# Down-projection tiles of a four-layer decoder on one core: twenty products of 256 columns become ten of 512, four stay

## The chip, the cores and the metric

The kernel runs on one core of one Trainium2 chip. The metric is the device time of one execution, in microseconds (us), and lower is better.

## The reference

Four post-norm layers over 256 tokens of 1024 channels. Each layer is a token mixer (forgetting attention, S5, mean pooling, forgetting attention again) and a SwiGLU feed-forward part with 2816 hidden channels; both are added to the residual and normalised. The change touches only the last factor of the feed-forward part.

```python
def swiglu(x, w1, w3, w2):
    return (jax.nn.silu(x @ w1) * (x @ w3)) @ w2

for i in range(DEPTH):                       # 4 layers
    m = mixer(h)                             # fox, s5, pool, fox
    h = layer_norm(DN_ALPHA * h + m, ln_g[i, 0], ln_b[i, 0])
    h = layer_norm(DN_ALPHA * h + swiglu(h, ffn_w1[i], ffn_w3[i], ffn_w2[i]), ln_g[i, 1], ln_b[i, 1])
```

## The kernel before, in words

**Split operands.** Every large product is made of three. Weights and activations are float32; each is split into a high part in the type that TensorE takes (fp32r) and a low part, the rest. The kernel sums high·high, high·low and low·high into the same PSUM bank.

**Weights.** They come as 370 tiles of 128 x 1024 floats in the order of their use. SyncE's queue brings a tile into one of four `raw` buffers; ScalarE writes its high part (line 617), VectorE its low part (line 1021), into a ring of places called `whi`/`wlo` (four places) and `ext` (up to four more, high and low). TensorE tells with the semaphore `w_used` when the last product of a tile is through, and the place is free.

**The feed-forward part.** The 2816 hidden channels are 22 chunks of 128. For a chunk c, `up1(c)` and `up3(c)` use one weight tile each: helper `fm` makes 24 products (8 blocks of 128 input channels, three products each, lines 1628 to 1630). In these, a 128 x 128 block of the *weight* is loaded into the array (the stationary operand), and 256 columns of the split activation `xboth`, all tokens, are streamed (the moving operand), into bank 4 or 5. ScalarE and VectorE make silu and gate, and split the result into `hhi` (line 703) and `hlo`, two buffers that alternate by chunk. The last two chunks of a layer have buffers of their own, `h3hi`/`h3lo` and `h4hi`/`h4lo`.

`down(c)` multiplies a chunk of h with its tile of w2 and adds to the accumulators of the layer, banks 0 to 3: tokens 0 to 127 in banks 0 and 1, tokens 128 to 255 in banks 2 and 3, 512 output channels in each. Here it is *h* that is loaded into the array, 128 hidden channels x 128 tokens, and the weight that is streamed. It goes through helper `tm_quarters` (line 1660): for each token half m, for each of the three pairs (a, w), four products of 256 columns, 24 in a tile. All other tiles of this orientation (attention's v and output, S5, the pool's output) go through `tm_half`, which makes the same sums with products of 512 columns, 6 for a token half. The last three chunks of a layer, four in the last layer, go through `tm_end`, also in products of 512 columns (line 1692), ordered bank by bank. So `tm_quarters` serves 19 chunks in each of the first three layers and 18 in the last.

**Order of the work.** It is written out by hand, per engine. In a layer's feed-forward part TensorE runs

```python
                for c in range(3, FCH):
                    up1(c)
                    up3(c)
                    if c < FCH - 3:
                        down(c - 1)
```

with `down(0)` and `down(1)` together ahead of it. `down` waits for its weight tile's low part (`w_lo`) and for h's low part (`hlo_ready`), and its last product raises `w_used`. In the first layer, eight blocks of transposes for S5 tables (line 1842) follow downs.

**Where things lie in SBUF.** The buffers are placed one behind another, and small fillers set their starts. Modulo 512 bytes, `whi`, `wlo`, `ext`, `ohi`, `olo` (the mixers' split outputs) and `h3hi` to `h4lo` start at 0; `xboth` starts at 448; `hhi` and `hlo` start at 64. A stationary operand of 128 floats is 512 bytes wide in each partition.

Of the kernel before, what the change touches and what calls it, by code (L numbers as in the profile page):

```python
# [27 lines left out]
P = 128  # L28
SEQ = 256
D = 1024  # L30
KC = D // P
TM = SEQ // P
HALF = 512
# [71 lines left out]
def build(nc, t, layers=DEPTH, last_ffn=True):  # L105
# [39 lines left out]
    with ExitStack() as ctx:  # L145
# [92 lines left out]
        def hi_of(c):  # L238

            p = place[c]  # L240
            return whi[:, p, :] if p < SPL else ext_hi[:, p - SPL, :] if p < SPL + EXT else far_hi[:, :]

        def lo_of(c):

            p = place[c]
            return wlo[:, p, :] if p < SPL else ext_lo[:, p - SPL, :] if p < SPL + EXT else far_lo[:, :]
# [1344 lines left out]
        def _(pe):  # L1591
            mm = nc.tensor.matmul
# [40 lines left out]
            def tm_half(c, m, a_hi, a_lo, banks, first, last=False, lo_ready=None):  # L1633

                cols = slice(m * P, (m + 1) * P)
                for j in range(2):
                    mm(banks[2 * m + j][:, :], a_hi[:, cols], hi_of(c)[:, j * HALF:(j + 1) * HALF], start=first, stop=False)  # L1637
                for j in range(2):
                    mm(banks[2 * m + j][:, :], a_hi[:, cols], lo_of(c)[:, j * HALF:(j + 1) * HALF], start=False, stop=False)  # L1639
                if lo_ready is not None:  # L1640
                    pe.wait_ge(xT_ready, lo_ready)
                for j in range(2):
                    ins = mm(banks[2 * m + j][:, :], a_lo[:, cols], hi_of(c)[:, j * HALF:(j + 1) * HALF], start=False, stop=last)  # L1643
                return ins
# [8 lines left out]

            def tm_quarters(c, a_hi, a_lo, banks, first):

                for m in range(TM):
                    cols = slice(m * P, (m + 1) * P)
                    for a, w, start in ((a_hi, hi_of(c), first), (a_hi, lo_of(c), False), (a_lo, hi_of(c), False)):
                        for q in range(4):
                            ins = mm(banks[2 * m + q // 2][:, q % 2 * SEQ:(q % 2 + 1) * SEQ], a[:, cols], w[:, q * SEQ:(q + 1) * SEQ],  # L1660
                                     start=start and q % 2 == 0, stop=False)
                return ins

            def tm_first(c, banks):
# [138 lines left out]
            def ffn(l, n):  # L1803
# [24 lines left out]
                def down(c):  # L1828
                    t = T0 + down_at(c)
                    pe.wait_ge(w_lo, t + 1)  # L1830
                    pe.wait_ge(hlo_ready, E0 + (2 if c < 2 else c + 1))
                    used(tm_quarters(t, hhi[:, c % 2, :], hlo[:, c % 2, :], acc, c == 0))
# [534 lines left out]
```

## Time and profile before

| | |
|---|---|
| median of three runs | 1169.89 us (1168.87 to 1171.18) |
| the profiled execution, its own time | 1169.65 us |
| its span, first to last instruction | 1167.9 us |
| TensorE busy | 1150.9 us, 99% |
| VectorE busy | 819.2 us, 70% |
| ScalarE busy | 601.4 us, 51% |
| matrix products (MATMUL records) | 9166 |
| mean granted TensorE clock | 0.999 |

The profiled execution's time is the span and 1.75 us around it. Matrix products are pipelined: the duration of a record (279 ns for 256 columns) is longer than the distance to the next start, so what a product costs is read from starts and not from durations. The timeline prints starts to 0.01 us; over the 24 products of a tile that is within half a nanosecond for each.

### The profile page before, as it was taken

The page shows a single profiled execution, that of the slowest core. Times are in us where ns is not written, and L with a number is a line of the kernel's source. Part 1 is how long each engine was busy: PE and PEld are TensorE (multiplying, and loading weights), DVE is VectorE, ACT ScalarE, POOL GpSimd, SP SyncE. Part 2 cuts the span into 40 slices and gives each one's busy share as a digit, 9 for nine tenths or more (in the row PEclk, how much of TensorE's full clock was granted, in tenths as well). Part 3 has the DMA queues.
Part 4 walks back from the last instruction along what each step waited for, and adds up shares of the span by engine and source line. Part 5 has one row for each costly group of instructions (what it writes and reads, how often), then busy time and mean ns, then how long its engine had stood idle before and what let it go on. Part 6 is the DMA issues. An engine that isn't in the chain of part 4 may idle for free.

```text
span 1167.9 us, 22245 instructions
## 1 busy us (share of the span) xinstructions
PE 1150.9 (99%) x9166; PEld 1068.3 (91%) x9166; DVE 819.2 (70%) x1263; ACT 601.4 (51%) x947; POOL 161.3 (14%) x212
## 2 busy tenths in 40 slices
PE   8999999999999999999999999999999999999997
PEld 7998899999977779999998899999989988999996
DVE  7789899989868687455466776554587768654545
ACT  6777544544445456354444555444438664644441
POOL 0650099002970000000000000000010000000000
PEclk9999999999999999999999999999999999999999
DMA  6676454554756558565654556656536334856540
GB/s 243 219 269 228 160 198 151 193 181 175 235 167 211 181 180 300 178 226 180 202 170 162 198 180 236 201 180 205 190 101 241 130 109 146 277 188 200 182 163 37
DMA packets 63981, 221.14 MB, mean 189 GB/s; under 512 B 8068, under 2 KB 9988, under 8 KB 63368
## 3 DMA queue, kind: packets, MB, share of 16 engines
q1 hardware_dynamic: 57224, 202.57, 50.8%
q0 software_dynamic: 5648, 15.73, 4.1%
q8 instruction: 73, 1.20, 0.4%
q10 hardware_dynamic: 1008, 1.41, 0.4%
q14 instruction: 28, 0.23, 0.1%
HBM read 211.03 MB, written 7.60 MB: 187 GB/s over the span
## 4 chain that ended last, share of the span: by engine, by line
PE 93%; DVE 4%; DMA 1%; ACT 1%; issue 1%; SPq 0%; DVEq 0%; ACTq 0%
PE bank L1660 18%; PE bank L1628 15%; PE bank L1629 15%; PE bank L1630 15%; PE bank L1758 5%; PE bank L1692 4%; PE bank L1637 3%; PE bank L1643 3%; PE bank L1639 3%; DMA raw<-in_w 1%; PE bank L1949 1%; PE bank L1608 1%; PE bank L1793 1%; PE bank L1931 1%; PE bank L1960 1%; PE bank L1948 1%
## 5 line engine op out<-in xcount | busy, mean ns | idle before, releaser
L1021 DVE TENSOR_TENSOR wlo<-raw,whi 128x1024 fp32r<-128x1024 f32 x227 | 288.3, 1277 | 61.2 <-ACT whi L617 60.3
L617 ACT ACTIVATE whi<-raw 128x1024 fp32r<-128x1024 f32 x227 | 239.0, 1056 | 76.5 <-PE bank L1660 29.1
L1628 PE MATMUL bank<-xboth,whi 128*128 128x256 f32 x936 | 261.3, 279 | 0.0
L1629 PE MATMUL bank<-xboth,whi 128*128 128x256 f32 x936 | 259.3, 277 | 0.0
L1630 PE MATMUL bank<-xboth,wlo 128*128 128x256 f32 x936 | 259.2, 277 | 0.0
L1021 DVE TENSOR_TENSOR ext<-raw,ext 128x1024 fp32r<-128x1024 f32 x142 | 172.3, 1222 | 42.3 <-ACT ext L617 42.1
L1628 PEld LDWEIGHTS bank<-xboth,whi 128*128 128x128 f32 x936 | 176.2, 188 | 1.1 <-issue 0.9
L1629 PEld LDWEIGHTS bank<-xboth,whi 128*128 128x128 f32 x936 | 175.9, 188 | 0.1
L1630 PEld LDWEIGHTS bank<-xboth,wlo 128*128 128x128 f32 x936 | 175.8, 188 | 0.0
L617 ACT ACTIVATE ext<-raw 128x1024 fp32r<-128x1024 f32 x142 | 148.9, 1056 | 45.8 <-PE bank L1660 22.5
L1628 PE MATMUL bank<-xboth,ext 128*128 128x256 f32 x600 | 167.2, 279 | 0.0
L1629 PE MATMUL bank<-xboth,ext 128*128 128x256 f32 x600 | 166.0, 277 | 0.0
L1630 PE MATMUL bank<-xboth,ext 128*128 128x256 f32 x600 | 166.0, 277 | 0.0
L1169 DVE TENSOR_TENSOR hval<-bank,silu 128x256 f32<-128x256 f32 x80 | 33.8, 423 | 159.8 <-PE bank L1630 159.7
L1628 PEld LDWEIGHTS bank<-xboth,ext 128*128 128x128 f32 x600 | 112.8, 188 | 0.9 <-issue 0.9
L1629 PEld LDWEIGHTS bank<-xboth,ext 128*128 128x128 f32 x600 | 112.8, 188 | 0.1
L1630 PEld LDWEIGHTS bank<-xboth,ext 128*128 128x128 f32 x600 | 112.7, 188 | 0.0
L703 ACT ACTIVATE hhi<-hval 128x256 fp32r<-128x256 f32 x72 | 30.0, 417 | 127.5 <-DVE hval L1169 125.4
L698 ACT ACTIVATE silu<-bank 128x256 f32<-128x256 f32 x80 | 30.5, 381 | 99.3 <-PE bank L1630 99.3
L584 POOL DMA_DIRECT2D slot<-in_ln_row x16 | 8.6, 545 | 446.0 <-DVE x_tm L1093 395.7
L1660 PE MATMUL bank<-ext,hhi 128*128 128x256 f32 x448 | 61.8, 281 | 0.0
L1660 PE MATMUL bank<-whi,hlo 128*128 128x256 f32 x376 | 59.6, 281 | 0.0
(383 smaller groups left out, 2036.1 us busy)
## 6 DMA issues: line engine op xcount, KB each, us to landing
raw<-in_w SPq DMA_DIRECT2D x370, 512.0 KB, 4.3
slot<-in_ln_row POOLq DMA_DIRECT2D x16, 512.0 KB, 5.1
toep<-slot POOLq DMA_DIRECT2D x8, 512.0 KB, 8.5
toepA<-toep SPq DMA_DIRECT2D x2, 1024.0 KB, 6.5
BT<-toep SPq DMA_DIRECT2D x2, 1024.0 KB, 7.3
x_tm<-in_x SPq DMA_DIRECT2D x2, 512.0 KB, 5.2
slot<-in_s_B SPq DMA_DIRECT2D x2, 512.0 KB, 5.6
slot<-in_s_C SPq DMA_DIRECT2D x2, 512.0 KB, 5.8
```

The costliest lines, as they stand in the source:

```text
L617: nc.scalar.activation(hi_of(c), raw[:, c % RAW, :], ACT.Copy).then_inc(w_hi, 1)
L1021: V.tensor_tensor(lo_of(c), raw[:, c % RAW, :], hi_of(c).bitcast(F32), ALU.subtract).then_inc(w_lo, 1)
L1169: V.tensor_tensor(hval[:, :], bank[5][:, 0:SEQ], silu[:, :], ALU.mult).then_inc(h_ready, 1)
L1628: mm(dst, wh, bhi[:, kc, :], start=(i == 0), stop=False)
L1629: mm(dst, wh, blo[:, kc, :], start=False, stop=False)
L1630: ins = mm(dst, wl, bhi[:, kc, :], start=False, stop=(i == len(chunks) - 1))
L1637: mm(banks[2 * m + j][:, :], a_hi[:, cols], hi_of(c)[:, j * HALF:(j + 1) * HALF], start=first, stop=False)
L1639: mm(banks[2 * m + j][:, :], a_hi[:, cols], lo_of(c)[:, j * HALF:(j + 1) * HALF], start=False, stop=False)
L1643: ins = mm(banks[2 * m + j][:, :], a_lo[:, cols], hi_of(c)[:, j * HALF:(j + 1) * HALF], start=False, stop=last)
L1660: ins = mm(banks[2 * m + q // 2][:, q % 2 * SEQ:(q % 2 + 1) * SEQ], a[:, cols], w[:, q * SEQ:(q + 1) * SEQ], start=start and q % 2 == 0, s ...
L1692: return mm(banks[b][:, :], (a_lo if lo_act else a_hi)[:, cols], (lo_of if lo_w else hi_of)(c)[:, half], start=False, stop=stop)
L1758: return mm(out, x[:, kc, m * P:(m + 1) * P], w[:, 0:4, kc * P:(kc + 1) * P], start=start, stop=stop)
```

## The change

`tm_quarters` is rewritten. The first token half goes through `tm_half`: six products of 512 columns. In the second, high·high and high·low are two products of 512 columns each, and low·high, the last, stays four products of 256 columns. The sums are the same, and added to each bank in the same order. A tile has 14 products in place of 24. Buffers, waits and the other engines' instructions are not touched.

```diff
             def tm_quarters(c, a_hi, a_lo, banks, first):
 
-                for m in range(TM):
-                    cols = slice(m * P, (m + 1) * P)
-                    for a, w, start in ((a_hi, hi_of(c), first), (a_hi, lo_of(c), False), (a_lo, hi_of(c), False)):
-                        for q in range(4):
-                            ins = mm(banks[2 * m + q // 2][:, q % 2 * SEQ:(q % 2 + 1) * SEQ], a[:, cols], w[:, q * SEQ:(q + 1) * SEQ],
-                                     start=start and q % 2 == 0, stop=False)
+                tm_half(c, 0, a_hi, a_lo, banks, first)
+                cols = slice(P, 2 * P)
+                for a, w, start in ((a_hi, hi_of(c), first), (a_hi, lo_of(c), False)):
+                    for j in range(2):
+                        mm(banks[2 + j][:, :], a[:, cols], w[:, j * HALF:(j + 1) * HALF], start=start, stop=False)
+                for q in range(4):
+                    ins = mm(banks[2 + q // 2][:, q % 2 * SEQ:(q % 2 + 1) * SEQ], a_lo[:, cols], hi_of(c)[:, q * SEQ:(q + 1) * SEQ],
+                             start=False, stop=False)
                 return ins
```

On TensorE, a down tile in the middle of the first layer's feed-forward part, with the end of the up tile ahead of it (lines 1628 to 1630) and the start of the next. Before:

```order
L1628 MATMUL bank<-xboth,whi 128x256
L1629 MATMUL bank<-xboth,whi 128x256
L1630 MATMUL bank<-xboth,wlo 128x256
L1660 MATMUL bank<-whi,hhi 128x256 x4
L1660 MATMUL bank<-wlo,hhi 128x256 x4
L1660 MATMUL bank<-whi,hlo 128x256 x4
L1660 MATMUL bank<-whi,hhi 128x256 x4
L1660 MATMUL bank<-wlo,hhi 128x256 x4
L1660 MATMUL bank<-whi,hlo 128x256 x4
L1628 MATMUL bank<-xboth,whi 128x256
L1629 MATMUL bank<-xboth,whi 128x256
```

With the change:

```order
L1628 MATMUL bank<-xboth,whi 128x256
L1629 MATMUL bank<-xboth,whi 128x256
L1630 MATMUL bank<-xboth,wlo 128x256
L1637 MATMUL bank<-whi,hhi 128x512 x2
L1639 MATMUL bank<-wlo,hhi 128x512 x2
L1643 MATMUL bank<-whi,hlo 128x512 x2
L1660 MATMUL bank<-whi,hhi 128x512 x2
L1660 MATMUL bank<-wlo,hhi 128x512 x2
L1662 MATMUL bank<-whi,hlo 128x256 x4
L1628 MATMUL bank<-xboth,whi 128x256
L1629 MATMUL bank<-xboth,whi 128x256
```

Nothing changes its place: five groups of four products of 256 columns have become five of two products of 512, and the group ahead of the next up tile is as it was. The lines 1637, 1639 and 1643 are those of `tm_half`.

## Rows read from the trace of the kernel before

**Rows 1.** The page: busy time of TensorE, and the chain that ended last
```profile
PE 1150.9 (99%) x9166; PEld 1068.3 (91%) x9166; DVE 819.2 (70%) x1263; ACT 601.4 (51%) x947; POOL 161.3 (14%) x212
...
PE bank L1660 18%; PE bank L1628 15%; PE bank L1629 15%; PE bank L1630 15%; PE bank L1758 5%; PE bank L1692 4%; PE bank L1637 3%; PE bank L1643 3%; PE bank L1639 3%; DMA raw<-in_w 1%; PE bank L1949 1%; PE bank L1608 1%; PE bank L1793 1%; PE bank L1931 1%; PE bank L1960 1%; PE bank L1948 1%
```
**Rows 2.** Waits of TensorE: us in total, times, longest; the two largest
```profile
PE bank L1608 <- DVE x_tm L1093: 2.7, 3, 1.1
PE bank L1668 <- ACT whi L617: 1.8, 1, 1.8
```
**Rows 3.** Line 1660, weight loads and products: ns min/median/max, first and last start
```profile
L1660 PEld LDWEIGHTS bank<-ext,hhi x448: 187/188/192, 459.7 to 1131.9; 128*128 128x128 f32 x150
L1660 PE MATMUL bank<-ext,hhi x448: 277/281/281, 459.8 to 1132.0; 128*128 128x256 f32 x150
...
L1660 PE MATMUL bank<-whi,hhi x376: 277/281/281, 145.3 to 1114.9; 128*128 128x256 f32 x188
...
L1660 PE MATMUL bank<-wlo,hhi x376: 281/281/281, 145.8 to 1115.4; 128*128 128x256 f32 x188
...
L1660 PE MATMUL bank<-whi,hlo x376: 281/281/283, 146.2 to 1115.9; 128*128 128x256 f32 x188
...
L1660 PE MATMUL bank<-ext,hlo x224: 281/281/282, 460.8 to 1132.5; 128*128 128x256 f32 x112
```
**Rows 4.** Timeline of PE (start us, us of the group): down tile, two up tiles, down
```profile
164.69 0.63 PE L1660 MATMUL bank<-whi,hhi 128*128 128x256 f32 x4
...
167.51 0.29 PE L1628 MATMUL bank<-xboth,whi 128*128 128x256 f32 x1
...
170.25 0.28 PE L1628 MATMUL bank<-xboth,whi 128*128 128x256 f32 x1
...
172.97 0.63 PE L1660 MATMUL bank<-whi,hhi 128*128 128x256 f32 x4
```
**Rows 5.** Timeline of PE, last layer's end: 512 columns, h stationary
```profile
1148.92 0.62 PE L1692 MATMUL bank<-ext,hhi 128*128 128x512 f32 x2
1149.37 0.40 PE L1692 MATMUL bank<-ext,hlo 128*128 128x512 f32 x1
1149.61 0.63 PE L1692 MATMUL bank<-ext,hhi 128*128 128x512 f32 x2
1150.08 0.39 PE L1692 MATMUL bank<-ext,hlo 128*128 128x512 f32 x1
1150.31 0.39 PE L1692 MATMUL bank<-whi,h3hi 128*128 128x512 f32 x1
...
1151.69 0.63 PE L1692 MATMUL bank<-ext,hhi 128*128 128x512 f32 x2
1152.16 0.40 PE L1692 MATMUL bank<-ext,hlo 128*128 128x512 f32 x1
...
1153.09 0.39 PE L1692 MATMUL bank<-whi,h3hi 128*128 128x512 f32 x1
```
**Rows 6.** Timeline of PE, attention output of the last layer: 512 columns, ohi stationary
```profile
963.19 0.61 PE L1639 MATMUL bank<-wlo,ohi 128*128 128x512 f32 x2
...
964.55 0.61 PE L1639 MATMUL bank<-wlo,ohi 128*128 128x512 f32 x2
...
966.82 0.62 PE L1692 MATMUL bank<-ext,ohi 128*128 128x512 f32 x2
967.27 0.39 PE L1692 MATMUL bank<-ext,olo 128*128 128x512 f32 x1
```
**Rows 7.** Timeline of PE, v to first q: tile of 512, then two up-like tiles
```profile
34.98 0.28 PE L1628 MATMUL bank<-xboth,whi 128*128 128x256 f32 x1
...
37.73 0.28 PE L1628 MATMUL bank<-xboth,whi 128*128 128x256 f32 x1
```
**Rows 8.** Timeline of PE, pool layer: 24 products of 256 between tiles of 512
```profile
652.05 0.62 PE L1643 MATMUL bank<-whi,xboth 128*128 128x512 f32 x2
652.51 0.28 PE L1628 MATMUL bank<-ohi,whi 128*128 128x256 f32 x1
...
655.39 0.40 PE L1637 MATMUL bank<-ext,xboth 128*128 128x512 f32 x1
```
**Rows 9.** Windows of those stretches: length, PE busy, PEclk, DMA share, GB/s
```profile
162.00:172.00 10.00, 10.00 (x90) 1.00 0.59 203
650.00:656.00 6.00, 6.00 (x39) 1.00 0.84 279
959.00:968.00 9.00, 9.00 (x45) 1.00 0.46 152
1148.92:1160.05 11.13, 11.13 (x50) 1.00 0.00 0
```

## The prediction, made before the changed kernel was run

> **What bounds the kernel now.** I read the page first. TensorE is busy for 1150.9 us of a span of 1167.9, and the chain that ended last runs through its products, 18% of it through line 1660, the one that changes [rows 1]. I then asked what TensorE waits for: the largest entries are 2.7 us and 1.8 us over the whole program, and neither is at line 1660 [rows 2]. So in the feed-forward parts no other engine or transfer is late. The time there is the sum of the distances between starts of products, and a nanosecond saved in a down tile is a nanosecond saved at the end. The granted clock is 1.00 in every stretch that I use, which is 2.4 GHz, so streaming alone is 256 / 2.4 = 106.7 ns or 512 / 2.4 = 213.3 ns [rows 9].
>
> The reader is to see next that starts say more than durations. A weight load's record takes 188 ns and a product's 281 [rows 3], yet a down tile, 24 products, goes from 164.69 to 167.51, in 2.82 us, so 117.5 ns a product [rows 4]. Loads and products overlap their neighbours. The excess over streaming is 10.8 ns a product. The up tiles beside it do better: the one right after the down tile takes 2.74 us (167.51 to 170.25), the second 2.72 (170.25 to 172.97), or 113.3 ns a product [rows 4].
>
> **How many tiles.** Line 1660 has 448 + 376 + 376 + 376 + 224 = 1800 products [rows 3], 24 in a tile, so 75 down tiles. They take 75 x 2.82 = 211.5 us, 18% of the span, which is what the chain says.
>
> **The change, part by part.**
>
> *Twenty products of 256 columns go.* At 117.5 ns each they are 2.350 us of a tile.
>
> *Ten of 512 columns come.* Before has no such product inside a down tile, but it has the same operands at a layer's end: `hhi` and `hlo` loaded, a tile of w2 streamed, 512 columns. The first six of them, right after an up tile, take 1148.92 to 1150.31 = 1.39 us; six later ones take 1151.69 to 1153.09 = 1.40 us, 233.3 ns each [rows 5]. These are the nearest rows, the same operands at the same addresses. A down tile also starts after an up tile, so I take 1.39 for its first six and 4 x 0.2333 = 0.933 for the next four: 2.323 us.
>
> *The bounds of this price.* From below: with `ohi` loaded, which starts at a multiple of 512 bytes, six take 963.19 to 964.55 = 1.36 us, 226.7 ns each [rows 6]; ten are 2.267 us. From above: the slowest pair with `hhi` is 0.47 us (1149.61 to 1150.08, 1151.69 to 1152.16), 235 ns a product [rows 5]; ten are 2.350 us, exactly what they replace. I take the value with h loaded, because the difference between the rows with `ohi` and with h goes with what is loaded, and that does not change.
>
> *Four of 256 stay.* 4 x 0.1175 = 0.470 us. They now follow a product of 512 columns. The price of that change of width is not in the trace for h; the nearest row is an up-like tile behind one of 512 columns: 34.98 to 37.73 = 2.75 us [rows 7], against 2.74 behind a down tile of 256 columns and 2.72 behind an up tile [rows 4]. So the change of width costs 0.01 us at most beyond what the change of operands costs anyway. Bounds: 0 and 0.03. I take 0.01.
>
> *The step to the next up tile.* The last four products are as before, so its first tile keeps its 2.74 us. Cost 0.
>
> *Everything else.* 750 products and 750 loads are no longer issued (a tile has 14, not 24); TensorE's records fall from 9166 to 8416. No wait, buffer, DMA or instruction of another engine is added. `down` still waits for `hlo_ready` and `w_lo`, which are never late [rows 2], and its last product still raises `w_used`, with 0.02 us less behind its first. Nothing hides this edit's terms, since the whole tile lies on the path that ends last; each counts in full. What could come late next is the weights' supply: three tiles of 512 KB in 164.69 to 172.97, 8.28 us, are 190 GB/s, and the same queues move 279 GB/s in another stretch [rows 4, 9]. 0.02 us in 8.28 do not touch that.
>
> *The sum.* A new tile: 1.39 + 0.933 + 0.470 + 0.01 = 2.803 us; an old one 2.82. The gain is 0.017 us, 0.02 at the precision of the starts, and x 75 = 1.5 us. Against the profiled execution's 1169.65 us (span 1167.9) that is 1168.2. The median of the runs stands 0.24 us above that execution, so I forecast 1169.89 - 1.5 = **1168.4 us**. 0.2% of it, 2.3 us, is about what a measurement of this kernel can tell from no change, so the forecast is "the same", a little on the fast side.
>
> **A rule weighed against the rows.** What a product costs beyond its streaming is 10.8 ns at 256 columns with h loaded and 233.3 - 213.3 = 20.0 ns at 512 [rows 4, 5]; for an aligned operand it is 226.7 - 213.3 = 13.4 ns at 512 [rows 6]. It almost doubles with the width, so it is nearly a share of the streaming (8 to 10%), and only some 2 ns a product (2 x 117.5 - 233.3 = 1.7) are a fixed price that wider products save. The Trainium skill, in "TensorE: Matmul & The Clock Gate", section "Wait — 56ns, not 53.3ns?", says that a warm product costs its columns over the clock and a fixed part behind decode, about 2.5 ns, whatever the width. By that figure, a tile would save 10 x 2.5 = 25 ns and the kernel 1.9 us; but by the same rule a tile of 24 would take 24 x 109.2 = 2620 ns, and the trace has 2820. So the rule does not account for most of the excess here. If that excess were fixed as well, the change would be worth more; this is rival B.
>
> **The rivals.**
>
> *A, aligned pace.* The products of 512 columns alternate banks, as in `tm_half`, where layer ends run several products in a row into one bank. If that order and not h's place set the 233.3 ns, they would run at 226.7 [rows 6]. A tile is 2.267 + 0.470 + 0.01 = 2.747 us, 0.073 less, 5.5 us in all: 1164.4 us. For it: the six rows of `ohi` at 226.7 are of `tm_half`, and those of h are not. Against: `ohi` keeps that pace in `tm_end`'s order too, where a pair takes 966.82 to 967.27 = 0.45 us, and h there takes 0.47 [rows 5, 6]. So far the pace follows the operand and not the order.
>
> *B, the excess is fixed per product.* A product of 512 would take 213.3 + 10.8 = 224.1 ns, a tile 10 x 0.2241 + 0.470 = 2.711 us, a gain of 0.109 or 8.2 us: 1161.7 us. For it: nothing but the rule quoted above, in whose terms this is. Against: no row of 512 columns anywhere is under 226 ns [rows 5, 6].
>
> *C, slower: the loads fall out of step and the following up tile pays.* In the pool layer, right behind products of 512 columns, 24 products of 256 take 652.51 to 655.39 = 2.88 us, 120 ns each, and never come back to 113.3 [rows 8]. If the mixed widths put the first up tile behind each down tile into that pace, it would take 2.88 and not 2.74: 0.14 x 75 = 10.5 us, less the 1.5 gained: 1178.9 us. It makes the kernel slower by over 0.2% from 0.05 us a tile on, that is from about eight products at 120 ns on. Against: in the pool's stretch `ohi` is streamed and not `xboth`, and behind 512 columns `xboth` recovers within the tile (2.75 us) [rows 7]; and the four narrow products lie between.
>
> *D, the upper bound.* Ten products at 235 ns and 0.02 for the change of width: 2.350 + 0.470 + 0.02 = 2.840, 0.02 more a tile: 1171.4 us. A matter of how six-product patterns fall, not of another mechanism.
>
> *E, the change does nothing at all,* because the tile's end is set by something else: 1169.9 us. Against: the waits.
>
> **How the numbers follow.** The forecast's case (a gain of 0 to 0.04 us a tile) has 0.62, A 0.12, B 0.05, C 0.09, D 0.08, E 0.04. In the forecast's case a fifth lies beyond 2.3 us of gain, 0.12; with A and B that makes faster 0.29. Slower is C and a quarter of D, 0.11. Same is the rest, 0.60. The range goes from 1164.3, which takes in A, to 1171.4, the bound D; B, C and some chance beyond are left out, under 2 in 10.
>
> **What would show it.** In the changed kernel's timeline a down tile should take 2.80 us (2.79 to 2.81) from the first product of line 1637 with h to the first of line 1628; the pair of products on lines 1637, 1639 and 1643 0.46 to 0.47 us; the last four 0.47 to 0.48; the up tiles behind 2.74 and 2.72. Pairs of 0.45 us would show A or B; an up tile of 2.8 or more, C. A wait of TensorE in the feed-forward parts of more than a microsecond in all, or a down tile outside 2.74 to 2.84 us, would make the reasoning wrong.

## The result, and the profile after

The changed kernel takes 1176.29 us, median of eight runs (1172.16 to 1177.33), against 1170.15 us for the kernel before (eight runs, 1167.84 to 1171.39). The ratio is 1.0046, 95% interval 1.0035 to 1.0056: slower by about 5.4 us, where 1.5 us less was forecast, and outside the range that ended at 1171.4. The profiled execution took 1174.88 us, its span is 1173.1, 5.2 more than before. The spread of the runs is worth a look: 5.2 us in eight, and 9.5 us (1170.61 to 1180.12) in twelve later ones, where the kernel before spreads over 3.6 us in eight.

The page of the changed kernel, answering to [rows 1], has the 8416 products that were expected, and TensorE is as busy as before:

```profile
PE 1157.6 (99%) x8416; PEld 1040.5 (89%) x8416; DVE 818.5 (70%) x1263; ACT 600.5 (51%) x947; POOL 160.2 (14%) x212
...
PE bank L1628 14%; PE bank L1629 14%; PE bank L1630 14%; PE bank L1660 6%; PE bank L1637 6%; PE bank L1643 6%; PE bank L1639 6%; PE bank L1760 5%; PE bank L1694 4%; PE bank L1662 3%; DMA raw<-in_w 2%; DVE wlo L1021 2%; PE bank L1608 1%; PE bank L1795 1%; DVE ext L1021 1%
```

So the time is still in TensorE's products, and the question is in which. The timeline of TensorE in the second layer (start us, us of the group), a down tile, the two up tiles and the next down tile, answers to [rows 4]:

```profile
466.53 0.62 PE L1637 MATMUL bank<-whi,hhi 128*128 128x512 f32 x2
...
468.86 0.64 PE L1662 MATMUL bank<-whi,hlo 128*128 128x256 f32 x4
469.33 0.29 PE L1628 MATMUL bank<-xboth,whi 128*128 128x256 f32 x1
...
472.07 0.28 PE L1628 MATMUL bank<-xboth,whi 128*128 128x256 f32 x1
...
474.79 0.39 PE L1637 MATMUL bank<-ext,hhi 128*128 128x512 f32 x1
```

Here all is as forecast: the down tile 2.80 us, the up tiles 2.74 and 2.72. The same view of the same execution in the third layer:

```profile
701.35 0.63 PE L1637 MATMUL bank<-ext,hhi 128*128 128x512 f32 x2
...
704.15 0.28 PE L1628 MATMUL bank<-xboth,ext 128*128 128x256 f32 x1
...
706.98 0.28 PE L1628 MATMUL bank<-xboth,whi 128*128 128x256 f32 x1
...
709.81 0.40 PE L1637 MATMUL bank<-whi,hhi 128*128 128x512 f32 x1
```

The down tile takes 2.80 us again, but both up tiles take 2.83: 118 ns a product in place of 113.3, for the same instructions with the same operands at the same clock. Every up tile of the feed-forward part behind a down tile of layers three and four is like this. In layer two none is: only its first takes 2.82 us, behind a stall, and the next is at 2.72 again. I call the two lengths the fast and the slow pace. A slow layer costs (0.09 + 0.11) us in each of its 19 passes, 3.8 us; two of them 7.6. The down tiles, 2.796 us where they were 2.823, give back 75 x 0.027 = 2.0.

A second, smaller loss is at two layers' starts. In these windows (length, PE busy, PEclk, DMA share, GB/s) TensorE was idle for 0.43 and 0.57 us:

```profile
448.00:457.00 9.00, 8.57 (x60) 1.00 0.89 297
692.00:701.00 9.00, 8.43 (x63) 1.00 0.86 279
```

There a weight tile lands late, ScalarE's split of it stands ahead of silu in its queue, and `up1(3)` waits for silu. The kernel before has no such wait in that profile, but the margin was small: in its third layer silu ended at 696.38 us and `up1(3)` began at 696.90. The rest, 5.2 - 7.6 + 2.0 - 1.0 = -1.4 us, lies elsewhere, mostly where nothing was changed: the first feed-forward part began 0.5 us earlier, and the stretch between the first and the second was 0.9 us shorter. In the first layer two things nearly cancel: three passes are slow, and end so at the first table transposes, but behind the transposes all up tiles are fast, where the kernel before has four slow pairs.

### The profile page after: what moved, and what is told of

Its sections match the earlier page's. It is cut to its first block, busy times and chain, and to the rows that moved or that the text cites. A ratio compares the mean times of both kernels' runs of the same rounds, so it can differ in the third digit from the quotient of the medians.

```text
span 1173.1 us, 20745 instructions
## 1 busy us (share of the span) xinstructions
PE 1157.6 (99%) x8416; PEld 1040.5 (89%) x8416; DVE 818.5 (70%) x1263; ACT 600.5 (51%) x947; POOL 160.2 (14%) x212
## 3 DMA queue, kind: packets, MB, share of 16 engines
q10 hardware_dynamic: 1008, 1.41, 0.4%
## 4 chain that ended last, share of the span: by engine, by line
PE 87%; DVE 8%; ACT 2%; DMA 2%; issue 1%; SPq 0%; ACTq 0%; DVEq 0%
PE bank L1628 14%; PE bank L1629 14%; PE bank L1630 14%; PE bank L1660 6%; PE bank L1637 6%; PE bank L1643 6%; PE bank L1639 6%; PE bank L1760 5%; PE bank L1694 4%; PE bank L1662 3%; DMA raw<-in_w 2%; DVE wlo L1021 2%; PE bank L1608 1%; PE bank L1795 1%; DVE ext L1021 1%
## 5 line engine op out<-in xcount | busy, mean ns | idle before, releaser
L627 ACT ACTIVATE xboth<-bank 128x256 fp32r<-128x256 f32 x64 | 21.2, 381 | 45.3 <-PE bank L1608 45.2
L1173 DVE TENSOR_TENSOR hlo<-hval,hhi 128x256 fp32r<-128x256 f32 x72 | 34.2, 475 | 0.0
```

## The experiments

**A second look at the same program.**

> The changed kernel once more, for a second profile of the same program. The first profile has up tiles (24 products of 256 columns) of two lengths: 2.72 to 2.74 us, as before the change, or 2.83 us, and in the third and fourth layer all of them are of the second kind. Theory I (inherited pace): the pace is set where a layer's feed-forward part begins, by how the starts happen to fall, and the new down tile hands it on. Then a second execution may have another set of layers at 2.83 us, and its time moves by some 4 us for each such layer. Theory II (the mixed tile itself is slow in these layers, by its places in the ring or by its addresses): the same layers and tiles at 2.83 us as in the first profile, and the same time, 1176 us.

Measured: 1175.99 us (twelve runs, ratio 1.0039, 1.0022 to 1.0055); the profiled execution 1171.54 us. Its third layer, slow in the first profile, is fast in this one:

```profile
709.83 0.62 PE L1637 MATMUL bank<-whi,hhi 128*128 128x512 f32 x2
...
712.63 0.29 PE L1628 MATMUL bank<-xboth,whi 128*128 128x256 f32 x1
...
715.37 0.28 PE L1628 MATMUL bank<-xboth,whi 128*128 128x256 f32 x1
...
718.09 0.39 PE L1637 MATMUL bank<-ext,hhi 128*128 128x512 f32 x1
```

2.80, 2.74 and 2.72 us. Of layers two to four only the last is slow in it, 38 up tiles of 38, and the profiled execution was 3.3 us quicker than the first. The program is the same to the byte, so addresses and ring places alone do not decide. Theory II falls.

**One old tile a layer.**

```diff
-                    used(tm_quarters(t, hhi[:, c % 2, :], hlo[:, c % 2, :], acc, c == 0))
+                    used((tm_narrow if c == 2 else tm_quarters)(t, hhi[:, c % 2, :], hlo[:, c % 2, :], acc, c == 0))
```

(`tm_narrow` is the old `tm_quarters`.)

> The change, but chunk 2 of each layer goes through the old down tile of 24 narrow products (4 tiles of 75). Theory I (inherited pace; 24 narrow products bring the following up tiles back to the fast pace, as every down tile did before, and 10 wide and 4 narrow ones do not): the up tiles of a layer are fast from chunk 4 on in all layers, some 8 us less than the changed kernel, 1168 to 1169.5 us. Theory II (the mixed tile makes the following up tile slow by itself): slow up tiles of 2.83 us come back behind the next mixed tile, about 1175 us.

Measured: 1168.63 us (eleven runs, 1166.72 to 1170.71), ratio to before 0.9981 (0.9971 to 0.9991). Timeline of TensorE at the start of its last layer; line 1672 is the old tile's:

```profile
998.43 0.28 PE L1628 MATMUL bank<-xboth,whi 128*128 128x256 f32 x1
...
1001.26 0.28 PE L1628 MATMUL bank<-xboth,whi 128*128 128x256 f32 x1
...
1004.09 0.63 PE L1672 MATMUL bank<-whi,hhi 128*128 128x256 f32 x4
...
1006.91 0.29 PE L1628 MATMUL bank<-xboth,whi 128*128 128x256 f32 x1
...
1009.65 0.28 PE L1628 MATMUL bank<-xboth,ext 128*128 128x256 f32 x1
...
1012.38 0.39 PE L1637 MATMUL bank<-ext,hhi 128*128 128x512 f32 x1
```

The layer starts slow (2.83, 2.83), one old tile of 2.82 us follows, and from then on the up tiles take 2.74 and 2.73, through 15 further mixed tiles. The first layer does the same; the second and third were fast when their old tile came, so the old tile ends the slow pace in two cases of two. A single mixed tile between up tiles neither makes the slow pace nor ends it. At a layer's start, where two of them follow each other, it is different (see the part on why the prediction was wrong). Replacing 4 tiles of 75 turned the change from 5 us slower into 2 us faster, which is about the gain that had been forecast for it.

**Kicks.** One idle product ahead of the down tile in two passes of layers 1 to 3 (counted from 0), in either kernel:

```diff
                     up3(c)
+                    if l > 0 and c in (8, 14):
+                        idle_products(7, 128)
```

> The changed kernel with one idle product of 128 columns (identity times a constant, into bank 7, which nothing reads) ahead of the down tiles in the passes of chunks 8 and 14 of layers 1 to 3; it adds under 0.3 us each. Theory I (inherited pace): the kick can move the starts from one pattern to the other, and what it leaves stays: the up tiles' length (2.72/2.74 or 2.83 us) changes at a kick and nowhere else within a layer. Theory II (places or addresses): the lengths do not care for the kicks.

Measured: 1172.95 us, one run. In the third layer, at chunk 8 (line 1730 is the kick, two records in the trace):

```profile
740.00 0.28 PE L1628 MATMUL bank<-xboth,whi 128*128 128x256 f32 x1
...
742.83 0.28 PE L1628 MATMUL bank<-xboth,ext 128*128 128x256 f32 x1
...
745.66 0.38 PE L1730 MATMUL bank<-cst 128*128 128x128 f32 x2
...
748.69 0.29 PE L1628 MATMUL bank<-xboth,ext 128*128 128x256 f32 x1
...
751.43 0.28 PE L1628 MATMUL bank<-xboth,ext 128*128 128x256 f32 x1
```

Up tiles of 2.83 us ahead of it, of 2.74 behind it, and fast to the layer's end. The last layer did the same. The second layer was fast, and both its kicks left it so. The pace changes at a kick and stays, as theory I has it; but the kick only led from slow to fast, which it had not said.

> The kernel before with the same kicks. Theory I: a down tile of 24 narrow products brings the fast pace back, so all up tiles of layers 1 to 3 behind a down tile stay at 2.74 and 2.72 us, kicks or not; the time is that of before and some 1 to 2 us. If up tiles of 2.83 us stay behind a kick here too, the old down tile does not restore the pace, and the theory falls.

Measured: 1172.27 us, one run. No up tile behind a kick is slow. This agrees, but tells less than hoped: no layer was in the slow pace when its kick came, so nothing had to be restored.

**h at multiples of 512 bytes.**

```diff
-        sb("behind_x", [P, 32])
+        sb("behind_x", [P, 16])
...
-        sb("behind_turn", [P, 4])
+        sb("behind_turn", [P, 20])
```

> The changed kernel with h's halves (and silu, hval and the tiles that share their place) 64 bytes lower, at multiples of 512 bytes; nothing else differs. If the pace of a wide product follows the address of what is loaded, as ohi's rows (226.7 ns) against h's (233.3 ns) say: the ten wide ones take 2.27 us and a down tile about 2.74 to 2.75 us in place of 2.80, 4 us less if the up tiles stay as they are in the changed kernel. If the address of h does not matter: down tiles of 2.80 us and no change. Open is what the up tiles do: fast throughout would give 1164 us, slow throughout 1180 us.

Measured: 1165.13 us (five runs, 1164.23 to 1165.60), ratio 0.9948 (0.9936 to 0.9960). Second layer:

```profile
498.53 0.63 PE L1637 MATMUL bank<-ext,hhi 128*128 128x512 f32 x2
...
500.81 0.64 PE L1662 MATMUL bank<-ext,hlo 128*128 128x256 f32 x4
501.29 0.29 PE L1628 MATMUL bank<-xboth,whi 128*128 128x256 f32 x1
...
504.03 0.28 PE L1628 MATMUL bank<-xboth,whi 128*128 128x256 f32 x1
```

The tile takes 2.76 us and the up tile 2.74; the ten wide products are 2.28 of it, 228 ns each, near [rows 6] and not [rows 5]. No layer of this execution stays slow. The second began with up tiles of 2.90 and 2.83 us behind a late start, and was fast from the next pass on, so this tile can end the slow pace; that is one case. The first and last layers, which began without delay, were fast from their first up tile.

A control moved silu and hval alike, and left h at 64 bytes above:

```diff
-        sb("behind_x", [P, 32])
+        sb("behind_x", [P, 16])
...
         hval = sb("hval", [P, SEQ])
+        sb("before_h", [P, 16])
```

> A control for the runs with h at 512: the changed kernel with silu and hval moved 64 bytes down as there, but h's halves left at 64 bytes above multiples of 512. If h's own address gave the 2.754 us tile and the return to the fast pace, this run is the changed kernel again: down tiles of 2.80 us, whole layers of up tiles at one pace or the other, 1170 to 1180 us by execution. If the neighbours' addresses did it: down tiles of 2.75 us and about 1165 us.

Measured: 1175.15 us, ratio 1.0039 (1.0022 to 1.0055). Down tiles of 2.80 us (706.08 to 708.88), layers two and four wholly slow. It is the changed kernel again, so h's own address is what counts, and not that of silu and hval. The kernel before got the same two changes of fillers as the first of these runs, its 24 narrow products kept:

> The kernel before (24 narrow products) with h's halves at multiples of 512 bytes. The pool layer's narrow products with operands at such addresses take 120 ns each, so if the address of what is loaded sets the pace: down tiles of 24 x 0.120 = 2.88 us and not 2.82, 4 us more, 1174 to 1175 us. If narrow products gain as the wide ones did: under 2.78 us and under 1168 us.

Measured: 1171.37 us (ten runs), ratio 1.0013 (0.9998 to 1.0028). The down tile is longer, as the first branch says, by 0.04 us and not 0.06; the time, for which it said 1174 to 1175 us, is not clear of no change:

```profile
508.45 0.63 PE L1660 MATMUL bank<-whi,hhi 128*128 128x256 f32 x4
...
511.31 0.29 PE L1628 MATMUL bank<-xboth,whi 128*128 128x256 f32 x1
```

2.86 us for 24, against 2.82 with h at 64. Inside the tile, narrow products lose by the address that wide ones gain by. The 75 tiles lose 2.8 us; 0.8 us come back in the first layer, where no up tile behind the transposes is slow in this run and four pairs were before. Whoever tried addresses with narrow products alone would find nothing to gain by leaving 64, and whoever tried widths at 64 alone would find narrow ones no worse.

**All products wide.**

```diff
-                    used(tm_quarters(t, hhi[:, c % 2, :], hlo[:, c % 2, :], acc, c == 0))
+                    used(tm(t, hhi[:, c % 2, :], hlo[:, c % 2, :], acc, c == 0, False))
```

> All products of a down tile 512 columns wide (12 of them), so the four last ones of 256 are gone as well. Theory I: a tile of 2.79 to 2.80 us, and the pace of the up tiles is handed on as well, so up tiles of 2.74/2.72 or 2.83 us by layer, time between 1168 and 1180 us by how many layers are slow. Theory III (it is the mix of widths in one tile that puts the loads out of step): up tiles 2.75 and 2.72 us everywhere, 1168 us.

Measured: 1174.14 us (seven runs, only 1173.24 to 1174.49), ratio 1.0022 (1.0012 to 1.0032). Last layer:

```profile
1037.17 0.28 PE L1628 MATMUL bank<-xboth,ext 128*128 128x256 f32 x1
...
1039.91 0.28 PE L1628 MATMUL bank<-xboth,ext 128*128 128x256 f32 x1
...
1045.42 0.28 PE L1628 MATMUL bank<-xboth,ext 128*128 128x256 f32 x1
...
1048.25 0.28 PE L1628 MATMUL bank<-xboth,whi 128*128 128x256 f32 x1
```

One pass has up tiles of 2.74 and 2.72 us, the next of 2.83 and 2.83, and so on to the layer's end, in layers two to four alike. Neither theory said this: the pace isn't handed on but changes side at each tile. If every execution has half of its passes slow, that would be why the time hardly varies. The same edit with h at multiples of 512 (both diffs together) is different again:

> h at multiples of 512 bytes and all 12 products of a down tile wide. Wide products took 226.7 ns with ohi: 12 are 2.72 us, and the four narrow ones at 120 ns each, a part of the 2.754 us of the run with h at 512, are gone: a down tile of 2.72 to 2.73. Theory I with up tiles fast throughout: 1163 to 1164 us, faster than the kernel with four narrow ones (1165.1 us). If the pace flips from tile to tile as it did with 12 wide products and h at 64: about 5 us more, 1168 us. This tells whether the four narrow ones are needed at that address.

Measured: 1175.23 us, ratio 1.0040 (1.0027 to 1.0053), a miss for both branches. Second layer:

```profile
501.13 0.61 PE L1637 MATMUL bank<-ext,hhi 128*128 128x512 f32 x2
...
503.85 0.28 PE L1628 MATMUL bank<-xboth,whi 128*128 128x256 f32 x1
...
506.68 0.28 PE L1628 MATMUL bank<-xboth,whi 128*128 128x256 f32 x1
```

The best down tile of all, 2.72 us, and the worst neighbour: up tiles of 2.83 us throughout nearly all of layers two to four. The two runs together show that a down tile must be judged with the two up tiles behind it. 0.10 us gained inside is worth less than the 0.20 lost behind.

**Where the narrow products stand, and how many.** First, 12 narrow ones in the second token half, behind six wide ones:

```diff
+                tm_half(c, 0, a_hi, a_lo, banks, first)
+                cols = slice(P, 2 * P)
+                for a, w, start in ((a_hi, hi_of(c), first), (a_hi, lo_of(c), False), (a_lo, hi_of(c), False)):
+                    for q in range(4):
```

> h at 64 bytes above, as in the kernel before; a down tile of 6 wide products (first token half), then 12 narrow ones (second half). Theory I says that a run of narrow h products at the end of the tile restores the fast pace and asks only how many it takes: 24 do, 4 do not. If 12 do: up tiles of 2.74 and 2.72 us throughout layers 1 to 3 from the second pass on, down tiles of 6 x 0.2333 + 12 x 0.1177 = 2.81 us, 1 us less than before in all, 1169 us. If they do not: whole layers with up tiles of 2.83 us, 1172 us or more.

Measured: 1176.69 us, ratio 1.0048 (1.0031 to 1.0066), the second branch. Layers two and four of the profiled execution are slow, layer three fast. In a slow one:

```profile
501.89 0.63 PE L1637 MATMUL bank<-ext,hhi 128*128 128x512 f32 x2
...
503.29 1.07 PE L1660 MATMUL bank<-ext,hhi 128*128 128x256 f32 x8
...
504.66 0.28 PE L1628 MATMUL bank<-xboth,whi 128*128 128x256 f32 x1
```

The 12 narrow products take 1.37 us, 114 ns each, where in [rows 4] they take 117.5: in the slow pace of the up tiles, narrow products of h behind wide ones are quick. In layer three, the fast one, they take 1.41 us and the tile 2.80. Each kind of tile has its own good side. That the two paces are two ways in which products and loads stand to each other would fit; no run measured it.

Then four narrow products at the tile's start, ten wide behind them:

```diff
+                for q in range(4):
+                    mm(banks[q // 2][:, q % 2 * SEQ:(q % 2 + 1) * SEQ], a_hi[:, 0:P], hi_of(c)[:, q * SEQ:(q + 1) * SEQ],
+                       start=first and q % 2 == 0, stop=False)
...
+                return tm_half(c, 1, a_hi, a_lo, banks, first)
```

> h at 64 bytes above; the same 10 wide and 4 narrow products in a down tile as in the changed kernel, but the narrow ones are the tile's first instead of its last. If what counts is how many products of each width a tile has, the picture is that of the changed kernel: whole layers at one pace. If what counts is how the tile ends: this tile ends in wide products as the all-wide one does, and the pace alternates from pass to pass (about half of the up tiles at 2.83 us, 1174 us). In both cases a down tile of 2.79 to 2.80 us.

Measured: 1169.57 us (ten runs, 1168.38 to 1171.57), ratio 0.9987 (0.9978 to 0.9996). Both branches missed: in layers two to four nothing alternates, and no layer stays slow. The second layer of this execution began with two slow passes behind a late start and was fast from the third on:

```profile
501.29 0.63 PE L1657 MATMUL bank<-ext,hhi 128*128 128x256 f32 x4
...
504.09 0.28 PE L1628 MATMUL bank<-xboth,whi 128*128 128x256 f32 x1
...
506.83 0.28 PE L1628 MATMUL bank<-xboth,whi 128*128 128x256 f32 x1
```

What the tiles that brought the pace back at 64 bytes, and kept it, have in common is that narrow products of h directly follow the narrow ones of the up tile: all 24, or the first four. Four or twelve behind wide products do not bring it back. This is a pattern and not yet a rule: the 24 did it twice, the first four once, at their second try. What is surer is that with the first four narrow both layers that began without delay began fast. The same ten and four as in the change, in the other order, give a kernel that is a little faster than before, by 0.13%.

**A version that beats both.** h at 512, eleven wide products and the last as two narrow ones:

```diff
+                mm(banks[2][:, :], a_lo[:, cols], hi_of(c)[:, 0:HALF], start=False, stop=False)
+                for q in range(2, 4):
+                    ins = mm(banks[3][:, q % 2 * SEQ:(q % 2 + 1) * SEQ], a_lo[:, cols], hi_of(c)[:, q * SEQ:(q + 1) * SEQ],
+                             start=False, stop=False)
```

> h at multiples of 512 bytes, 11 wide products and the last one as 2 narrow ones. In the run with four narrow ones at that address their distances are 113, 119, 120, 120 ns in the trace, and the up tiles behind are fast; in the run with none the up tiles are slow (1175 us). If two are enough: the tile is 2.754 less 2 x 0.120 and plus 0.227, 2.74 us, up tiles 2.74 and 2.72, 1 us less than the run with four (1165.1): 1164 us. If not: up tiles of 2.83 us and some 1173 to 1175 us.

Measured: 1163.66 us (five runs, 1161.98 to 1164.30), ratio 0.9933 (0.9921 to 0.9945).

```profile
499.43 0.63 PE L1637 MATMUL bank<-ext,hhi 128*128 128x512 f32 x2
...
502.17 0.29 PE L1628 MATMUL bank<-xboth,whi 128*128 128x256 f32 x1
...
504.90 0.28 PE L1628 MATMUL bank<-xboth,whi 128*128 128x256 f32 x1
...
507.62 0.39 PE L1637 MATMUL bank<-whi,hhi 128*128 128x512 f32 x1
```

A down tile of 2.74 us, up tiles of 2.73 and 2.72. (2.82 - 2.74) x 75 = 6.0 us of the 7.8 that the ratio says. The spans of the two profiled executions, 1167.9 and 1161.9, differ by 6.0; the rest I did not trace.

## Why the prediction was wrong

- **What bounds the kernel** was right: TensorE's products, before and after.
- **The price of ten wide products** was right. 2.323 us was forecast; 466.53 to 468.86 is 2.33. With the four narrow ones the tile is 2.80 us, as forecast, in the fast and in the slow layers. The gain of a tile was forecast as 0.017 us and entered as 0.02, 1.5 us in all; it is 0.027, or 2.0. (The excess over streaming, given as 8 to 10%, is 9 to 10% with h by the prediction's own numbers, and 6% for the aligned operand.)
- **"The step to the next up tile ... keeps its 2.74 us. Cost 0."** This is the step that failed. The last four products are the same instructions as before, and that was taken for enough. They are not at the same distances: in a fast layer the last three stand 117 to 120 ns from the next start, in a slow layer 113. The pace of an up tile depends on a state that runs through the down tile. Between up tiles the old tile ended the slow pace in both cases seen, the new one passes it on, and two new ones in a row make it (below). The term was 0, for the first up tile and, unsaid, for the second; it measured up to 0.20 us a pass, 3.8 us a layer. In the executions profiled of the changed kernel one or two whole layers paid it, and three passes of the first layer.
- **"`down` still waits for `hlo_ready` and `w_lo`, which are never late."** Nearly right; the wait that came, 1.0 us in all, was for silu behind a late weight tile. It comes and goes from one execution to another. Whether the change makes it more frequent is not settled, but the profiles lean that way: in the three with 24 narrow products a tile, one start of six in layers two and three is late, by 0.05 us; in the other eleven 16 of 22 are, by 0.07 to 1.75 us.
- **Rival C** named the loss and half of its place, the first up tile at 120 ns a product behind mixed widths, and priced it at 0.14 us a pass. It measured 0.09 there and 0.11 in the second up tile, 118 ns a product, in the slow layers only. C had a chance of 0.09, for the wrong reason: it took the pool layer as evidence, where other operands are streamed. Better evidence was in the trace of before, and I didn't look there. Behind the table transposes of the first layer (line 1842), the timeline of the kernel before has

```profile
175.80 1.03 PE L1842 MATMUL bank<-cst,BT 128*128 128x128 f32 x8
176.59 0.37 PE L1628 MATMUL bank<-xboth,whi 128*128 128x256 f32 x1
...
179.50 0.28 PE L1628 MATMUL bank<-xboth,whi 128*128 128x256 f32 x1
...
182.33 0.28 PE L1660 MATMUL bank<-whi,hhi 128*128 128x256 f32 x1
```

  The up tile from 179.50 takes 2.83 us, not 2.72. So the slow pace was there, entered without any wide product, behind four of the eight blocks of transposes. Each time it was gone in the next pass, but there an old down tile and a block of transposes stood between, so this trace can't tell which of them ended it. The question "what ends it?" would have pointed to the edit's risk; it took the run with one old tile a layer to answer it.
- **Rivals A and B** do not hold at h's place, where the wide product kept 233 ns. A's number came true when h was moved: it is the address, as the rows with `ohi` and h had said.
- **The weighed rule.** The Trainium skill ("TensorE: Matmul & The Clock Gate", section "Wait — 56ns, not 53.3ns?") gives a fixed 2.5 ns a warm product. Inside the tile, ten products fewer saved 0.027 us, about its 10 x 2.5 ns; the 118 and 113.3 ns of one and the same product are a difference that a price by width alone can't make.

**Where the slow pace comes from.** The traces show what sets the state where a layer begins. There `down(0)` and `down(1)` follow each other without an up tile between. The start of the last layer in the changed kernel's first profile, from the end of `down(0)` on:

```profile
998.67 0.64 PE L1662 MATMUL bank<-ext,hlo 128*128 128x256 f32 x4
999.14 0.63 PE L1637 MATMUL bank<-ext,hhi 128*128 128x512 f32 x2
...
1001.48 0.62 PE L1662 MATMUL bank<-ext,hlo 128*128 128x256 f32 x4
1001.93 0.28 PE L1628 MATMUL bank<-xboth,whi 128*128 128x256 f32 x1
...
1004.76 0.28 PE L1628 MATMUL bank<-xboth,whi 128*128 128x256 f32 x1
```

The four narrow products take 0.47 us in `down(0)`, as in the fast layers' tiles, and 0.45 in `down(1)`, as in the layers at the slow pace; the up tile behind takes 2.83. Five profiles have layers that start with two of these tiles (the two of the changed kernel, the run with one old tile a layer, the one with kicks, and the control), 20 starts in all. In 12 the first up tile follows at once, and all 12 are slow. In the other 8 it begins 0.07 to 1.75 us late; 7 are fast, and one, the third layer of the first profile, is slow. The kernel before, with or without kicks, has 7 starts without delay, all fast. In seven of the 20 starts, this one among them, `down(0)` has the distances of a fast layer's tile and `down(1)` those of a slow one. So two mixed tiles in a row make the slow pace and single ones between up tiles hand it on, while the fast layers are those that started late: the wait of 0.43 us in layer two, counted above as a loss, most likely saved 3.8. Much of the spread may come from this; no run delayed a layer's start on purpose. With four narrow products first, or with h at a multiple of 512 and a short narrow tail, every start without delay is fast.

What the state is stays open. The traces show two stable distances between starts for the same products, and what leads from one to the other. A collision of the reads of what is loaded and of what is streamed would fit the part that addresses play. This is only argued; no run here measured it.

## What to carry to other kernels

Cost a change of a product's shape over the whole period in which it stands, the unchanged tiles behind it included. Where the same instructions have two lengths in a trace, find what enters the slow one and what ends it before removing anything, since an inefficient-looking tile may be what restores the fast one. Look also at the places where the changed tile follows itself: there the loss began. And try width and address together: here each alone looked like no gain or a loss, and both with a short narrow tail gave 0.7%.

## What the runs showed of the hardware that I had not expected

- The same product of 256 columns at a granted clock of 1.00 has two stable distances, 113.3 and 118 ns, kept for whole layers (the slow one from 695.6 to 847.8 us in the changed kernel's first profile), and two executions of one program differ in them.
- At a layer's start, two tiles of ten wide and four narrow products in a row, with h at 64 bytes above a multiple of 512, left the slow distance in 12 starts of 12 without delay; two tiles of 24 narrow ones left the fast one in 7 of 7.
- Twelve wide products between up tiles switch the pace at every pass of layers two to four with h at 64 bytes above a multiple of 512 (2.74 and 2.83 us in turn), and hold it slow with h at a multiple (2.83).
- The start of the loaded operand sets a wide product's mean distance, at the two places tried: about 227 to 228 ns at a multiple of 512 bytes, 233 ns at 64 above. For 24 narrow ones it goes the other way, 2.86 us against 2.82.
